# Rotary turns, half exchange and index-key shift as copies inside SBUF in a two-layer hybrid block

## The reference

```python
score[t, s] = sum_h iw[t, h] * relu(iq[t, h, :] . ik[s, :])
```

```python
def partial_rope(x, pos):
    ...
    rot = jnp.concatenate([x1 * cos - x2 * sin, x2 * cos + x1 * sin], axis=-1)
    return jnp.concatenate([rot, x[..., ROPE_DIM:]], axis=-1)

blocks = kv[:, idx] + pos_emb[:, None, :]
hid = jax.nn.silu(jnp.einsum('bnlgd,ldh->bgnh', blocks, w1))
```

## Time and profile before

| | us |
|---|---|
| median of 3 runs | 891.28 |
| lowest, highest run | 890.68, 891.84 |
| profiled execution, first to last instruction (span) | 888.7 |
| median less span | 2.6 |
| PE busy | 876.6 |
| DVE busy | 587.4 |

### The profile page before, as it was taken

The page is one execution under the profiler, slowest core; times in us unless marked ns, Lnnn a source line. Parts: engine busy times, 40 slices in busy tenths (PEclk is TensorE's granted clock), DMA queues, the critical chain, the costliest instruction groups (busy, mean ns, idle before and its releaser), DMA issues.

```text
span 888.7 us, 13795 instructions
## 1 busy us (share of the span) xinstructions
PE 876.6 (99%) x5624; PEld 759.9 (86%) x5624; DVE 587.4 (66%) x898; ACT 441.7 (50%) x644; POOL 51.2 (6%) x78
## 2 busy tenths in 40 slices
PE   8999999999999999999999999999999999999997
PEld 6888999898999888888889999877788888888885
DVE  5775664565656756555686997956477777777544
ACT  6644444753345544544485652466254555555442
POOL 1000000000020110000020015200000100000000
PEclk9999999999999999999999999999999999999999
DMA  9757644456454554555747683412455556665541
GB/s 299 233 190 229 221 144 142 143 165 183 127 182 153 188 174 158 171 187 193 268 140 253 156 178 95 144 49 49 143 190 179 184 184 189 190 190 190 166 166 48
DMA packets 127813, 151.67 MB, mean 171 GB/s; under 512 B 16983, under 2 KB 93142, under 8 KB 127750
## 3 DMA queue, kind: packets, MB, share of 16 engines
q1 hardware_dynamic: 127466, 150.44, 54.4%
q10 hardware_dynamic: 220, 0.28, 0.1%
q0 software_dynamic: 64, 0.07, 0.0%
HBM read 148.67 MB, written 3.68 MB: 171 GB/s over the span
## 4 chain that ended last, share of the span: by engine, by line
PE 88%; DVE 8%; ACT 2%; issue 1%; DMA 1%; POOL 0%; POOLq 0%; SPq 0%; ACTq 0%; DVEq 0%
PE bank L519 18%; PE bank L521 18%; PE bank L520 18%; PE bank L1354 9%; PE bank L545 5%; PE bank L1355 5%; PE bank L546 3%; DVE w_lo L2136 2%; DVE arena L2548 1%; PE bank L1014 1%; PE bank L748 1%; PE bank L728 1%; PE bank L847 1%; DMA arena<-in_x 1%; PE bank L708 0%
## 5 line engine op out<-in xcount | busy, mean ns | idle before, releaser
L2136 DVE TENSOR_TENSOR w_lo<-ring,w_hi 128x2048 fp32r<-128x2048 f32 (+1 forms) x134 | 298.2, 2230 | 125.7 <-ACT w_hi L1561 125.3
L1561 ACT ACTIVATE w_hi<-ring 128x2048 fp32r<-128x2048 f32 (+1 forms) x134 | 248.9, 1860 | 98.4 <-PE bank L521 72.4
L519 PE MATMUL bank<-h_both,w_hi 128*128 128x256 f32 x488 | 140.3, 287 | 0.3 <-DVE w_lo L2136 0.3
L520 PE MATMUL bank<-h_both,w_hi 128*128 128x256 f32 x488 | 138.0, 283 | 0.0
L521 PE MATMUL bank<-h_both,w_lo 128*128 128x256 f32 x488 | 138.0, 283 | 0.0
L1354 PE MATMUL bank<-h_both,w_hi 128*128 128x512 f32 x352 | 124.8, 399 | 0.2 <-issue 0.2
L1355 PE MATMUL bank<-h_both,w_lo 128*128 128x256 f32 x352 | 98.8, 281 | 0.0
L519 PEld LDWEIGHTS bank<-h_both,w_hi 128*128 128x128 f32 x488 | 93.5, 192 | 2.3 <-issue 1.4
L520 PEld LDWEIGHTS bank<-h_both,w_hi 128*128 128x128 f32 x488 | 93.6, 192 | 0.1
L521 PEld LDWEIGHTS bank<-h_both,w_lo 128*128 128x128 f32 x488 | 93.5, 192 | 0.0
L1354 PEld LDWEIGHTS bank<-h_both,w_hi 128*128 128x128 f32 x352 | 66.1, 188 | 16.7 <-issue 0.4
(11 more groups left out here) (387 smaller groups left out, 1553.7 us busy)
## 6 DMA issues: line engine op xcount, KB each, us to landing
ring<-in_w_in SPq DMA_DIRECT2D x59, 1024.0 KB, 5.2
ring<-in_w_gate_up SPq DMA_DIRECT2D x44, 512.0 KB, 4.7
ring<-in_w_down SPq DMA_DIRECT2D x10, 1024.0 KB, 5.1
ring<-in_w_mem_kv SPq DMA_DIRECT2D x8, 1024.0 KB, 9.2
ring<-in_w_gla_out SPq DMA_DIRECT2D x4, 1024.0 KB, 5.0
ring<-in_w_x_out SPq DMA_DIRECT2D x4, 1024.0 KB, 5.2
ring<-in_w_dsa_out SPq DMA_DIRECT2D x4, 1024.0 KB, 5.7
ring<-in_w_o SPq DMA_DIRECT2D x4, 1024.0 KB, 5.0
```

What stands on the lines that cost most here:

```text
L519: mm(o, ah, bh, start=start, stop=False, skip_group_check=True)
L520: mm(o, ah, bl, start=False, stop=False, skip_group_check=True)
L1561: act(w_hi[:, k % NHI, at:m], ring[:, order.index(name) % NSLOT, at:m], ACT.Copy)\
L2136: tt_(w_lo[:, i, at:m], ring[:, i, at:m], w_hi[:, k % NHI, at:m].bitcast(F), ALU.subtract)\
```

## The change

The constant matrices `rope` and `selg` go, and the sign of the turn goes into the sine table (negative on the first eight rows of each group). No matmul turns rows any more. SP copies rows from SBUF to SBUF instead: eight rows at a time into `rotated` (in the scratch `prob`, cleared once by POOL), 64 rows at a time into `swapped` (in `probT`), and the index key into `ikT[0]`. These copies are issued by SP in its own order, after the load of the unit that takes the slot of `kcks`, `kwvc`, `nq0` or `nq1`, with waits for ACT's eviction and for the first rotary addition. The index-key copy is issued after the load of `mk3`. DVE multiplies the copies by the sines in place. The first rotation on DVE now stands ahead of the norm columns, the second and the value blocks between the norm columns' input and `qg`, the key blocks after `nA`. On POOL the first two cosine products stand ahead of the power, the third behind it. PE waits for `ik_moved` before the index scores, and for `blocks_ready` before the hidden rows.

```diff
@@ constants
-            sin[a] = sin[b] = np.sin(ang[:, i])
-            rot[b, a] = -1.0
-            rot[a, b] = 1.0
+            sin[b] = np.sin(ang[:, i])
+            sin[a] = -sin[b]
...
+        swapped = tiled(probT_at, 2, S)
+        rotated = [prob[:, i % 3, 0:n * S].rearrange("p (a b) -> p a b", a=n) for i, n in enumerate((2, 1, 2, 2))]
@@ TensorE
             bank = open_bank("ik2")
-            mm(bank[0:64, 0:256], ident[64:128, 64:128], smallT[64:128, :], start=True, stop=True)
...
-            pe.wait_ge(*read("ik2"))
+            pe.wait_ge(signal("ik_moved"), 16)
...
             head_products("qg", 0)
-            pe.wait_ge(*read("kwvc"))
-            rope_turn("r0", 0, 2)
-            rope_turn("r1", 2, 1)
             project_channels("nq1", h_parts)
             head_transposes("kk", 4)
-            pe.wait_ge(*read("nq0"))
-            rope_turn("r2", 4, 2)
             pe.wait_ge(signal("silu_done"), 6)
             head_transposes("vt", 8)
-            pe.wait_ge(*read("nq1"))
-            rope_turn("r3", 6, 2)
-            pe.wait_ge(signal("rope_done"), 1)
-            for kv, tile in ((0, 0), (1, 3)):
...
             bank = open_bank("hid")
-            for kv in range(2):
-                pe.wait_ge(*read(f"sh{kv}"))
+            pe.wait_ge(signal("blocks_ready"), 2)
@@ SyncE
+            turned_units = {"kcks": (0, 0, 2), "kwvc": (1, 2, 1), "nq0": (2, 4, 2), "nq1": (3, 6, 2)}
...
+                if name == "mk3":
+                    sp.wait_ge(*read("small"))
+                    sp.dma_start(ikT[0], smallT[64:128, :]).then_inc(signal("ik_moved"), 16)
+                if i >= NSLOT and order[i - NSLOT] in turned_units:
+                    n, a, count = turned_units[order[i - NSLOT]]
+                    sp.wait_ge(*read(order[i - NSLOT]))
+                    if n == 0:
+                        sp.wait_ge(signal("turned_zero"), 1)
+                    if n > 1:
+                        sp.wait_ge(signal("rope_done"), 1)
+                    for g in range(2):
+                        for half in range(2):
+                            to, of = 64 * g + 8 * half, 64 * g + 8 - 8 * half
+                            sp.dma_start(rotated[n][to:to + 8, :, :], ns[of:of + 8, a:a + count, :])\
+                              .then_inc(signal(f"turned{n}"), 16)
+                    if n in (1, 2):
+                        kv, tile = (1, 3) if n == 1 else (0, 0)
+                        for q in range(2):
+                            sp.dma_start(swapped[64 * q:64 * q + 64, kv, :], ns[64 - 64 * q:128 - 64 * q, tile, :])\
+                              .then_inc(signal(f"swapped{kv}"), 16)
@@ ScalarE
-            sc.wait_ge(*full("ik2"))
-            act(ikT[0], bank_of("ik2")[0:64, 0:256], ACT.Copy).then_inc(signal("ik2"), 1)
@@ GpSimd
+            gp.wait_ge(*full("gtok"))
+            nc.gpsimd.memset(prob, 0.0).then_inc(signal("turned_zero"), 1)
...
+            def rope_cos(i, a, n):
+                gp.wait_ge(signal(f"turned{i}"), 64)
...
+            rope_cos(0, 0, 2)
+            rope_cos(1, 2, 1)
             gp.wait_ge(*read("ss"))
             nc.gpsimd.tensor_tensor(norm_cols, norm_cols, mhalf.broadcast_to([128, 16]), ALU.pow)\
                 .then_inc(signal("norm_cols"), 1)
...
-            rope_cos("r0", 0, 2)
-            rope_cos("r1", 2, 1)
-            rope_cos("r2", 4, 2)
+            rope_cos(2, 4, 2)
@@ VectorE
             def rope_sin(i, a, n):
-                bank_ready(f"r{i}")
+                lows(splits_by[("kg1", "ss", "kk1", "vt1")[i]] + 2)
+                ve.wait_ge(signal(f"turned{i}"), 64)
                 sinb = const("sin").unsqueeze(1).broadcast_to([128, n, S])
...
+                tt_(rotated[i], rotated[i], sinb, ALU.mult).then_inc(signal("rope_sin"), 1)
...
+            def compressed_blocks(kv):
+
+                ve.wait_ge(signal(f"swapped{kv}"), 32)
+                for g in range(2):
+                    for q in range(2):
+                        r = slice(64 * q, 64 * q + 64)
+                        own = ns[r, 3 * kv, :] if q == g else swapped[r, kv, :]
+                        t_ = own.rearrange("p (n s) -> p s n", s=16)
+                        dst = cblk[kv][r, :, 15 * g:15 * g + 15]
...
+                ins.then_inc(signal("blocks_ready"), 1)
...
+            rope_sin(0, 0, 2)
+            rope_add(0, 0, 2)
             bank_ready("ss")
             tsc(norm_cols, bank_of("ss")[:, 0:16], 4 * EPS, None, ALU.add).then_inc(reader("ss"), 1)
+            rope_sin(1, 2, 1)
+            compressed_blocks(1)
+            rope_add(1, 2, 1)
             for t in range(TT):
                 bank_ready(f"qg{t}")
...
             ins.then_inc(signal("nA_ready"), 1)
-            rope_sin(0, 0, 2)
-            rope_sin(1, 2, 1)
-            rope_add(0, 0, 2)
-            rope_add(1, 2, 1)
+            compressed_blocks(0)
```

More of the change, by code:

```diff
@@ L56, in _const_columns @@
     for name, width in (("ident", 128), ("diag3", 384), ("keep", S), ("chunk", 128), ("bucket", 383), ("pad", 1),
-                        ("lev", 6 * 64), ("id64", 64), ("chunk64", 64), ("after", 128), ("rope", 128), ("cos", S), ("sin", S), ("selg", 256),
+                        ("lev", 6 * 64), ("id64", 64), ("chunk64", 64), ("after", 128), ("cos", S), ("sin", S),
                         ("ones", 1),
@@ L95, in shape_constants @@
     put("diag3", np.concatenate([diag, np.zeros((128, 128)), diag], 1))
-    rot = np.zeros((128, 128), np.float32)
     cos = np.ones((128, S), np.float32)
@@ L104, in shape_constants @@
             cos[a] = cos[b] = np.cos(ang[:, i])
-            sin[a] = sin[b] = np.sin(ang[:, i])
-            rot[b, a] = -1.0
-            rot[a, b] = 1.0
-    put("rope", rot)
+            sin[b] = np.sin(ang[:, i])
+            sin[a] = -sin[b]
     put("cos", cos)
     put("sin", sin)
[L111 to L116, removed]
     put("ones", np.ones((128, 1)))
@@ L986, in _ @@
             project_channels("kwvc", h_parts)
-            def rope_turn(name, a, n):
-                bank = open_bank(name)
-                done(name, mm(bank[:, 0:256 * n], const("rope"), ns[:, a:a + n, :], start=True, stop=True))
             def head_products(name, a):
@@ L2073, in _ @@
             nc.gpsimd.tensor_tensor(egc, egc, cv[:, 0:4, :], ALU.mult).then_inc(signal("q_decayed"), 1)
+            def rope_cos(i, a, n):
+                gp.wait_ge(signal(f"turned{i}"), 64)
+                cosb = const("cos").unsqueeze(1).broadcast_to([128, n, S])
+                nc.gpsimd.tensor_tensor(ns[:, a:a + n, :], ns[:, a:a + n, :], cosb, ALU.mult).then_inc(signal("rope_cos"), 1)
+            rope_cos(0, 0, 2)
+            rope_cos(1, 2, 1)
             gp.wait_ge(*read("ss"))
@@ L2095, in _ @@
             level_mask(1)
-            rope_cos("r3", 6, 2)
+            rope_cos(3, 6, 2)
             gp.wait_ge(*read("qg1"))
@@ L2206, in _ @@
             ve.wait_ge(*full("ik2"))
-            ve.wait_ge(signal("ik2"), 1)
             tsc(iw.rearrange("p a b -> p (a b)"), bank_of("ik2")[:, 256:272], IDX_H ** -0.5 * IDX_D ** -0.5, None, ALU.mult)\
@@ L2570, in rope_sin @@
             def rope_sin(i, a, n):
-                bank_ready(f"r{i}")
+                lows(splits_by[("kg1", "ss", "kk1", "vt1")[i]] + 2)
+                ve.wait_ge(signal(f"turned{i}"), 64)
                 sinb = const("sin").unsqueeze(1).broadcast_to([128, n, S])
-                tmp = prob[:, i % 3, 0:n * S].rearrange("p (a b) -> p a b", a=n)
-                tt_(tmp, bank_of(f"r{i}")[:, 0:n * S].rearrange("p (a b) -> p a b", a=n), sinb, ALU.mult)\
-                    .then_inc(reader(f"r{i}"), 1)
+                tt_(rotated[i], rotated[i], sinb, ALU.mult).then_inc(signal("rope_sin"), 1)
             def rope_add(i, a, n):
-                tmp = prob[:, i % 3, 0:n * S].rearrange("p (a b) -> p a b", a=n)
-                ve.wait_ge(*read(f"r{i}"))
+                ve.wait_ge(signal("rope_sin"), i + 1)
                 ve.wait_ge(signal("rope_cos"), i + 1)
-                tt_(ns[:, a:a + n, :], ns[:, a:a + n, :], tmp, ALU.add).then_inc(signal("rope_done"), 1)
+                tt_(ns[:, a:a + n, :], ns[:, a:a + n, :], rotated[i], ALU.add).then_inc(signal("rope_done"), 1)
+            def compressed_blocks(kv):
[6 more added lines that the diff above has]
+                        dst = cblk[kv][r, :, 15 * g:15 * g + 15]
+                        for half in range(2):
+                            ins = tt_(dst[:, 8 * half:8 * half + 8, :], t_[:, q::2, half:half + 15],
+                                      cmp_pos[kv][r, 8 * half:8 * half + 8].unsqueeze(2).broadcast_to([64, 8, 15]), ALU.add)
+                ins.then_inc(signal("blocks_ready"), 1)
             lows(splits_by["kg1"] + 2)
@@ L2594, in _ @@
                 tt_(qkT[:, s, :], qkT[:, s, :], by_chunk(f"qg{t}"), ALU.mult).then_inc(reader(f"qg{t}"), 1)
-            lows(splits_by["r1"] + 1)
+            lows(splits_by["qg1"] + 1)
             ve.wait_ge(signal("norm_cols"), 1)
@@ L2623, in _ @@
```

## The result

The changed kernel takes 900.67 us (median of four runs, 899.01 to 901.29) beside 891.19 for the kernel before in the same session: 1.0105 times as long, 95% interval 1.0093 to 1.0116. It is slower, as forecast, but by 9.5 us where 4.1 were forecast. The profiled execution is the fastest of the four (span 897.2, 8.5 above).

The account below looks back on a forecast made before the run. PE, busy 99% of the span, was taken to bound the kernel, with DVE ending the rotary stage. Span 888.7 + 4.6 + 1.3 - 1.8 = 892.8, plus 2.6 from span to median, gave 895.4 us; range 891.6 to 902.6.

Parts of the forecast that it names:

- Index-key copy: Before the index scores: the SBUF copy queues behind the mk3 load, so PE starts at 33.2 instead of 28.62, +4.6 us.
- Clock in that wait: PE's clock probably falls while it waits for the index key; +1.3 us, the middle of 0 and 2.6.
- Rotary copies, there in time: Rotary stage: SP's copies land just after the load ahead of each, before DVE can use them.
- Clearing: POOL's clearing of the scratch rows falls where POOL and the queue are idle and costs nothing.
- the lock: A DVE operation with two SBUF tensors and a POOL product exclude each other for a whole instruction; the waiting one goes next.
- DVE's gain: Rotary stage: DVE saves 1.87 + 1.95 + 0.5 and loses 2.54 to POOL's masks, a gain of 1.8 us.
- Taking turns with the two masks: Rotary stage: DVE's key block additions out of SBUF wait for both POOL mask products, costing 2.54 us.
- PE is then ahead and waits for DVE's transposed matrix as now: End of rotary stage: about 4.7 us of removed PE matmuls are no gain yet, since DVE ends the stage.
- the 2.6 added for what lies around the span: Whole kernel: the earlier median, 891.28, lies 2.6 us above the profiled span; the same was added to the forecast.
- the first (POOL's power holds the lock): Rotary stage: POOL's 2.93 us power also excludes DVE's two-SBUF-input operations, delaying the value blocks; 901.7 us, chance 0.25.
- The second (no turns): Rotary stage: DVE keeps the interface through a row of operations, so 2.54 isn't paid; 892.9 or 891.6 us, chance 0.23.
- The third (the copy is hidden): Index key: the copy lands before PE needs it, so neither 4.6 nor 1.3 is paid; 889.5 us, chance 0.07.

## Why the prediction was right in direction and too small

- **Index-key copy, +4.6: right, in part by luck.** 4.55 with the clock kept. That it stands behind mk3 in SP's queue is shown by the run from ACT's queue. But it landed at 34.0, not 33.1, since mk3 itself landed at 20.03 + 13.6 = 33.6, not 32.9. With the clock kept the scores started 5.2 us late; that they then took 3.44 us instead of 4.01 gave 0.6 back.
- **Clock in that wait, +1.3 (0 to 2.6): mechanism right, too small.** 1.7 in the profiled execution, 2.6 between medians, up to 7.9 - 4.5 = 3.4 in another trace: at the upper bound or above it. How long the low level lasts differs between executions (to 38 us in the changed kernel's, past 40 in the one with the key blocks moved).
- **Rotary copies, there in time: right.** Four of eight partitions took SP 2.75 us to issue, 0.7 each where 0.38 was taken, but DVE waited for none of them.
- **Clearing "where POOL and the queue are idle: nothing": wrong.** POOL was idle, DVE was not: 0.8 us. I had read the lock out of the rows and applied it to products alone.
- **DVE's gain, -1.8: the sign right, mis-sized, 1.0.** Taking turns with the two masks cost 4.44 - 2.57 = 1.9, where 2.54 was taken: 0.6 less. Against it, the eight block additions behind the power cost 2.55 us out of SBUF, where 1.95 out of PSUM (half of the 3.90 in the earlier trace rows) was taken: 0.6 more. And the third rotary product, which now reads SBUF, was held by POOL's mask of `qkT` (558.45 to 559.74), 1.34 for 0.67: 0.7 more. 1.8 + 0.6 - 0.6 - 0.7 leaves 1.1.
- **"PE is then ahead and waits for DVE's transposed matrix as now": the step that failed most.** 4.7 us of matmuls were taken from PE and priced at nothing because DVE ends the stage. They became one wait of 4.5 us, and the clock fell in it: 2.5 us in the profiled execution, 2.5 to 3.7 in the five traces with this wait (9.83 to 11.05 us from the first level to the third, 7.32 before), 3.4 between medians. I had the mechanism in hand for the first wait and didn't apply it to the second.

In the profiled execution the missing terms are 0.4 + 0.8 + 0.8 + 2.5 = 4.5 us, and 892.8 + 4.5 = 897.3 against a span of 897.2. The medians are 5.3 apart, 0.9 more. The time of every recorded run is 1.8 to 1.9 us above its span, so of the 2.6 added for what lies around the span 0.8 was that the profiled execution of the kernel before was quicker than its median; that of the changed kernel is 1.7 quicker than its own. Longer low clocks in the other executions would do this; it isn't shown.

Of the rivals, the first (POOL's power holds the lock) gave 901.7, near the time, and is refuted: eight block additions take 2.57 us beside a power of 3.05 us and 2.55 beside nothing. That the time lies inside the stated range is luck, since only this rival had drawn the range so far up. The second (no turns) is refuted by the 4.44. The third (the copy is hidden) became true as soon as the copy had another queue. The estimate of 2.2 us beside it comes from a fit that the Trainium skill (DMA: Bandwidth & Descriptors, section Anatomy of one DMA) gives for transfers issued by GpSimd; this copy was SP's and took 9.7 us, and from ACT's queue 5.7.

## What to carry to other kernels

Work taken from PE while another engine holds it up isn't free: if what is left becomes one stand (2.5 us and more here), PE's clock can fall, and the next work pays; either bring the other engine forward or fill the wait. A small copy inside SBUF belongs in a queue with nothing large ahead of it (5.7 us to landing, 9.7 behind a load). Before an operation is put "where POOL is idle", look at what DVE does at that moment.

## What the runs showed of the hardware

- A POOL zeroing (1.39 us) held two DVE products of 256 columns by a per-partition scalar, 1.44 us for 0.62. The Trainium skill, GPSIMD Engine Reference, section Key points, names such contention for DVE instructions in a 2-port mode, which would fit a product with a single SBUF input; no run here shows the mode.
- A power on 16 columns, 3.05 us long on POOL, held nothing on DVE.
- In these traces the instruction that comes second is held: a 2.29 us split kept the masks waiting at full speed (two masks 4.51 us), while short DVE operations let POOL's in between them.
- PE's granted clock fell to half (0.50 to 0.53) at or behind the waits of 6.1, 4.5, 3.0 and 2.5 us, and stayed at 1.00 at those of 0.2 to 1.2 us.
